# Moving the operands of a two-block transformer kernel's matmuls from 192 to 224 bytes behind its weights, modulo 512

## What is computed

```python
# first block
x = x + hybrid_mixer(x, ...)       # rmsnorm(x) @ w_in, gated delta rule and attention, @ w_out
x = x + cross_attention(x, mem, ...)
x = x + conv_ffn(x, ...)           # (silu(conv(h @ w_gate) + b) * (h @ w_up)) @ w_down, d_ff = 5632
x = rmsnorm(x, final_norm_g)
# second block, layer 0, then layer 1
x = layernorm(ALPHA * x + mamba2_mixer(x, a_w_in, ..., a_w_out))
x = layernorm(ALPHA * x + swa_mixer(x, k_sh, v_sh, b_w_in, ..., b_w_out))
```

## Time and profile before

| | us |
|---|---|
| three runs | 2512.45, 2535.52, 2535.87 |
| their median | 2535.52 |
| the profiled execution's own time | 2531.28 |
| its span from the first to the last instruction | 2529.5 |
| PE busy in the span | 2465.5 (97%) |
| VectorE, ScalarE, GpSimd busy | 1748.3, 1213.0, 410.0 |
| mean granted TensorE clock | 0.995 of full |

### The profile page before, as it was taken

The page is one execution under the profiler, slowest core; times in us unless marked ns, Lnnn a source line. Parts: engine busy times, 40 slices in busy tenths (PEclk is TensorE's granted clock), DMA queues, the critical chain, the costliest instruction groups (busy, mean ns, idle before and its releaser), DMA issues.

```text
span 2529.5 us, 51575 instructions
## 1 busy us (share of the span) xinstructions
PE 2465.5 (97%) x20854; PEld 2402.8 (95%) x20854; DVE 1748.3 (69%) x2781; ACT 1213.0 (48%) x1906; POOL 410.0 (16%) x543
## 2 busy tenths in 40 slices
PE   7999999999899999999999999999999999899997
PEld 7999999989899999999999999999999999899997
DVE  6677655685766655655656887767787777777777
ACT  6334344444544444444444554445445544556554
POOL 1233200050200000000002301240101112510102
PEclk9999999999999999999999999999999999999999
DMA  6433345554455556556555654445455444444443
GB/s 221 151 117 123 120 142 171 179 173 161 147 187 190 186 168 202 190 168 206 187 168 184 191 187 155 158 152 183 152 167 166 161 148 159 156 155 154 146 162 122
DMA packets 124502, 418.35 MB, mean 165 GB/s; under 512 B 13796, under 2 KB 17644, under 8 KB 124012
## 3 DMA queue, kind: packets, MB, share of 16 engines
q1 hardware_dynamic: 124268, 415.06, 49.7%
HBM read 412.37 MB, written 3.68 MB: 164 GB/s over the span
## 4 chain that ended last, share of the span: by engine, by line
PE 89%; DVE 5%; ACT 3%; issue 2%; POOL 1%; DMA 0%; SPq 0%; ACTq 0%; DVEq 0%; POOLq 0%
PE b L737 27%; PE b L739 26%; PE b L738 26%; DVE WL L1601 2%; PE b L716 1%; PE b L1084 1%; PE b L852 1%; ACT WH L1204 1%; PE b L865 1%; PE b L1095 1%; DVE t1s L1699 1%; DVE XT L2208 0%; ACT XH L1210 0%; PE b L1143 0%; DVE XT L1793 0%
## 5 line engine op out<-in xcount | busy, mean ns | idle before, releaser
L737 PE MATMUL b<-XH,WH 128*128 128x256 f32 x4224 | 1209.2, 286 | 20.1 <-DVE WL L1601 15.6
L738 PE MATMUL b<-XL,WH 128*128 128x256 f32 x4224 | 1179.9, 279 | 0.0
L739 PE MATMUL b<-XH,WL 128*128 128x256 f32 x4224 | 1179.9, 279 | 0.0
L1204 ACT ACTIVATE WH<-WR 128x1024 fp32r<-128x1024 f32 (+2 forms) x811 | 816.7, 1011 | 576.0 <-PE b L739 570.7
L1601 DVE TENSOR_TENSOR WL<-WR,WH 128x1024 fp32r<-128x1024 f32 (+2 forms) x811 | 977.9, 1215 | 15.7 <-ACT WH L1204 15.4
L737 PEld LDWEIGHTS b<-XH,WH 128*128 128x128 f32 x4224 | 796.2, 188 | 34.2 <-issue 19.5
L738 PEld LDWEIGHTS b<-XL,WH 128*128 128x128 f32 x4224 | 802.2, 190 | 4.0 <-issue 3.3
L739 PEld LDWEIGHTS b<-XH,WL 128*128 128x128 f32 x4224 | 796.7, 189 | 0.0
L737 PE MATMUL b<-OH,WH 128*128 128x256 f32 x1680 | 479.8, 286 | 3.8 <-DVE WL L1601 2.4
L738 PE MATMUL b<-OL,WH 128*128 128x256 f32 x1680 | 469.2, 279 | 0.0
L739 PE MATMUL b<-OH,WL 128*128 128x256 f32 x1680 | 469.1, 279 | 0.0
(11 more groups left out here) (388 smaller groups left out, 2206.4 us busy)
## 6 DMA issues: line engine op xcount, KB each, us to landing
WR<-a_w_in SPq DMA_DIRECT2D x160, 512.0 KB, 3.6
WR<-w_in SPq DMA_DIRECT2D x112, 512.0 KB, 3.6
WR<-w_gate SPq DMA_DIRECT2D x88, 512.0 KB, 3.9
WR<-w_up SPq DMA_DIRECT2D x88, 512.0 KB, 3.9
WR<-a_w_out SPq DMA_DIRECT2D x64, 512.0 KB, 3.5
WR<-b_w_in SPq DMA_DIRECT2D x64, 512.0 KB, 3.6
WR<-w_down SPq DMA_DIRECT2D x64, 384.0 KB, 3.5
WR<-w_down SPq DMA_DIRECT2D x64, 320.0 KB, 2.9
```

The source lines that it names most:

```text
L737: mm(ps, WH[:, slot, at:at + P], xh, start=(k == 0), stop=False)
L738: mm(ps, WH[:, slot, at:at + P], xl, start=False, stop=False)
L739: m = mm(ps, WL[:, slot, at:at + P], xh, start=False, stop=(k == p["kt"] - 1))
L1204: act.activation(WH[:, s, 0:n], WR[:, r, 0:n], ACT.Copy).then_inc(*act_w.up(i))
```

## The change

The unused buffer `apart` grows from 48 to 56 float32 per partition, 192 to 224 bytes. Everything allocated behind it (`XH`, `XL`, `OH`, `OL`, `OX`, `t2x`, `t2s`, `t1s`, `KM`, `VM`, `par`, `con` and the rest) lies 32 bytes further back in the partition; `WR`, `WH`, `WL` and `XT` stay. The distance between weight tile and moving tile is then 224 modulo 512, and `XH` starts at byte 86368, a multiple of 32 but not of 64. On every engine (PE, DVE, ACT, POOL, SP) the instructions, their order and their waits are the same as before.

```diff
     XT = sb("XT", [P, 16, S])
-    sb("apart", [P, 48])
+    sb("apart", [P, 56])
     XH = sb("XH", [P, 16, S], F32R)
```

## The result

The changed kernel takes 2568.51 us (median of four runs, 2565.75 to 2569.95), the kernel before 2533.92 beside it (2512.45 to 2535.87). The ratio is 1.0187, with a 95% interval of 1.0124 to 1.0249: slower by 1.9%. The forecast was 2504 us and faster; its range ended at 2566.

What follows compares the result with a forecast made beforehand. PE streaming its matmuls was taken as the bound. The long stretch turning fast gives 27.4 us, all other terms 0: 2531.3 - 27.4 = 2503.9, forecast 2504 us, range 2474 to 2566 (the forecast's own 2490 to 2511).

Steps and rivals of the forecast that it cites:

- What bounds the kernel: PE streaming its matmuls; one ns on each of 18,432 product matmuls is 18.4 us, 0.7% of the span.
- Two rhythms: Same product matmuls run at 117.7 or about 113.4 ns; a stretch that has found its rhythm keeps it.
- the long stretch: 685 to 1427 us, 6302 matmuls, slow rhythm from one end to the other in the profile before.
- it gives back 27.4 us: 685 to 1427 us turning fast: 6302 x 4.35 ns = 27.4 us gained, taken in full; bounds nothing or 27.4.
- two readers meet: Weight load and matmul hinder each other where their distance modulo 512 makes them meet; 32 bytes moves that some 7 ns.
- All other products: The other 12,130 product matmuls keep their mix of rhythms: 0; bounds over all products 53.5 us gained, 26.7 lost.
- Rival 2: All products slow at the new distance, including stretches at 1870 and 2455 us: 26.7 us lost, 2558 us; chance 0.23.
- third, slower rhythm: Within the worse-distance case: one more step of 4.35 ns on all products, 80 us more; nothing in the rows for it.
- The multiple of 64: Moving tiles would no longer start at a multiple of 64 bytes, which could cost one more access per matmul.
- Rival 1: Address has no say; the break ahead of a stretch chooses its rhythm: 2531 us, chance 0.33 including a mix as before.
- The floor of 109 ns: Skill's gap N / 2.4 + 2.5 ns for 256 columns, some 130 us less than now; no stretch came below 113.
- The feed keeps up: Splits and loads follow a faster PE (24 matmuls 2.72 us, DVE's split 1.22 us), so nothing of 27.4 us is lost.

Runs made afterwards that it cites:

- both back: Changed kernel with the weights also 32 bytes further back, so distance 192 again and `XH` still off 64: 2524.55 us, ratio 1.0002.
- 224 on 64: Kernel before with weights 32 and moving operands 64 bytes further back, distance 224, `XH` on a multiple of 64: 2568.76 us, ratio 1.0204.
- the last kernel: Kernel before with weights and moving operands both 16 bytes further, distance still 192: 2495.95 us, ratio 0.9880.

## Why the prediction was wrong

*What bounds the kernel, and one ns per matmul being 18.4 us*: right. The kernels of this study with the same instructions are ordered in time as they are in mean spacing, where the spacings differ by more than 0.1 ns, and the product of the spacing's difference and the count gives the time: 17,700 x (118.3 - 116.1) = 39 us for the change (37.8 measured in the span), 17,700 x (119.85 - 116.1) = 66 for distance 0 (63.2).

*Two rhythms, and a stretch keeps the one it has*: right for 192. The two heaps of the runs came from the long stretch, as the prediction took it: 27.4 us was its term, and the medians of the heaps lie 28.6 apart.

*"If the new distance lets it run fast, it gives back 27.4 us ... I take the full 27.4"*: this is the step that failed. The long stretch gave nothing back and took 3.5 us more. The prediction took for granted that the two rhythms seen at 192 are the only two, and that an address merely picks one. Each distance has rhythms of its own; 224 has one, at 118.3, and neither of the two seen. That the distance has a say is borne out; that two readers meet at a place set by it is not shown by any run, and even if it were so, it could not give a sign: nothing in a trace of one distance tells where the good one is. The runs at 192 in the lower heap were evidence that 192 is good, and they were read as evidence that leaving it would help.

*"All other products ... I leave their mix as it is: 0"*: the second term that failed, and with 34 us the larger part of the loss. No reason was given for the 0. A change of distance that was to turn the rhythm of one stretch had to be expected to act on the others too; it took the fast rhythm from all of them.

*Rival 2, the new distance is the worse one*: this came true, by its mechanism (the stretches fast before lose it), with its price too small: 26.7 us against 37.8. It had the slow rhythm of 117.7 take over; the one that did is 118.3, some 0.6 ns more on each of 17,700 spacings, 11 us. And the share of fast matmuls was under-estimated: it took one third from mean durations, in which a few long ones count as slow; by the starts it was 39%, 6977 spacings that were 4.15 ns under the others, 29 us. Together 40, less the idle time that shrank by 4, is 36 of the 37.8 us. It named a third, slower rhythm too, priced it at one more step of 4.35 ns and found nothing in the rows for it. One of its own rows spoke for one: L1021 (64-column weights) stands at 277/280/285 in the earlier trace rows, which is not the 281 of the slow rhythm that it was taken for, and its first 23 spacings average 119.0 ns in the trace of before. The sentence against it, that a rhythm steady over 162 matmuls isn't close to its edge, is refuted: steadiness in time says nothing of tolerance in the address. 4 bytes off 192 it is gone.

*The multiple of 64*: named for rival 2, refuted (both back, 224 on 64).

*Rival 1, the address has no say*: refuted. Half of it holds: at 192 both rhythms occur, and something other than the address picks. With PE alone the same instructions took from 113.3 to 123.4 ns by the address and the entry alone. The Trainium skill, "SBUF — State Buffer", section "Who interferes with whom", gives PE two independent read ports and says that it never waits on anyone. What the prediction drew from it, that the distance of PE's two operands is of no consequence, does not hold here. That no other engine holds PE up is not contradicted: PE alone shows the kernel's rhythms.

*The floor of 109 ns*: no settled stretch of this study came below 113.3. The Trainium skill, "TensorE: Matmul & The Clock Gate", section "Back-to-back issue gap", gives the formula N / 2.4 + 2.5 for a single isolated matmul, not as the floor of a stream with weight loads, so the prediction's word floor goes beyond it.

*The feed keeps up*: right. At 113.3 ns the idle time ahead of the first line of the products from `MV` is 24.9 us, against 20.1 + 3.8 ahead of L737 for the same products before.

## What to carry to other kernels

Where TensorE is bound by a stream of equal matmuls with a weight load each, measure the spacing of their starts in gapless stretches before anything else, and sweep the start addresses of weights and moving operand against each other in a kernel with PE alone: a hundred stretches fit in one run of 2 ms. Sweep both the distance and the common offset, in steps of 16 bytes, behind several entries and more than once each, and take a place that is fast in all of them, not one that is fast once. Then copy both, distance and offset, into the kernel: the distance of 112 alone, without its offset, gave the kernel 2589 us instead of 2499. A trace at one address pair cannot tell which way to move, so such an edit shouldn't be forecast from it with more than even chances either way.

## What the runs showed of the hardware

The spacing of float32r matmuls of 256 columns with a weight load of 128 columns each took one of a few values, 113.3, 116.7, 117.8, 118.3 to 119.3, 120.0 and 121.7 ns among them, at full clock and with nothing else running. They follow the distance of the two operands, nearly always alike for distances 256 bytes apart, and their place modulo 32 (moved by 32 bytes together they kept their rhythm at 112 and 192, moved by 16 they did not). At some distances one address pair has two rhythms, and a stretch keeps the one in which it settled near its start; what picks it was not found. The lowest was 113.3, whatever the address. What in the memory or in PE's reads makes it so was not found: the fall of the cost with the load's width, which two readers in each other's way would suggest, did not appear. Also open is why the short stretches of the last kernel stay at 114.6 ns on average from 100 to 685 us, where PE alone settled at 113.3 behind every entry; the first matmuls behind each break, slower in every run, are one part of it.
